# RWKV block inversion: each level product moves only 32 of 64 columns

## The reference, cut to what matters

```python
def step(S, inp):
    r_t, d_t, k_t, v_t, kk_t, a_t = inp
    sa = jnp.einsum('bhij,bhj->bhi', S, -kk_t)
    S = (S * d_t[:, :, None, :] + sa[..., None] * (kk_t * a_t)[:, :, None, :]
         + v_t[..., None] * k_t[:, :, None, :])
    return S, jnp.einsum('bhij,bhj->bhi', S, r_t)
```

## Time and profile before

| | |
|---|---|
| median of 3 runs | 2666.61 us (2660.39 to 2673.18) |
| profiled execution, time | 2664.87 us |
| its span | 2663.1 us |
| TensorE matmuls, busy | 2542.4 us, 95% |
| VectorE, busy | 1375.4 us, 52% |
| ScalarE, busy | 1082.2 us, 41% |
| GpSimd, busy | 1630.0 us, 61% |
| granted TensorE clock, mean | 0.976 |

### The profile page before, as it was taken

How to read it: one execution, slowest core, us unless ns; L and a number is a source line. 1 busy time by engine, 2 the same in 40 slices (tenths; PEclk the granted TensorE clock), 3 DMA queues, 4 the chain that set the end, 5 groups by cost and what they waited for, 6 DMA issues and landing times.

```text
span 2663.1 us, 56828 instructions
## 1 busy us (share of the span) xinstructions
PE 2542.4 (95%) x23437; PEld 2350.3 (88%) x23437; DVE 1375.4 (52%) x2444; ACT 1082.2 (41%) x1752; POOL 1630.0 (61%) x844
## 2 busy tenths in 40 slices
PE   5899999889979999999999999999989999999997
PEld 3799999657757999999999999999988888888887
DVE  0450355773336455995574010010177777777777
ACT  1333433341223434444333333333444554555555
POOL 0366677012225776888655777777667777777763
PEclk9899999889989999999999999999999999999999
DMA  9987845567855444445555654654588999999884
GB/s 374 395 290 268 274 170 171 183 249 251 261 194 218 170 165 140 158 159 180 180 176 193 239 196 159 257 194 168 192 309 307 323 374 321 332 358 318 311 305 131
DMA packets 213561, 639.92 MB, mean 240 GB/s; under 512 B 16520, under 2 KB 26264, under 8 KB 183832
## 3 DMA queue, kind: packets, MB, share of 16 engines
q1 hardware_dynamic: 176712, 514.54, 55.6%
q0 software_dynamic: 27472, 97.56, 10.1%
q10 hardware_dynamic: 9216, 25.53, 2.4%
HBM read 605.61 MB, written 31.97 MB: 239 GB/s over the span
## 4 chain that ended last, share of the span: by engine, by line
PE 69%; issue 12%; POOL 9%; DVE 5%; DMA 4%; ACT 1%; POOLq 0%; DVEq 0%; ACTq 0%; SPq 0%
PE bank L929 68%; POOL ring_lo L806 8%; DMA kept<-in_peer_v 3%; DVE ring_lo L2791 1%; DVE act_hl L2788 1%; ACT hi_peer L1690 0%; PE bank L932 0%; DVE staged L2853 0%; POOL ring_lo L813 0%; DMA staged<-in_w_ada 0%; DVE staged L2373 0%; DVE staged L2397 0%; ACT act_hl L1690 0%; ACT staged L1687 0%; DVE staged L2781 0%
## 5 line engine op out<-in xcount | busy, mean ns | idle before, releaser
L1690 ACT ACTIVATE hi_peer<-kept 128x1024 fp32r<-128x1024 f32 x544 | 559.2, 1053 | 906.2 <-PE bank L929 775.4
L806 POOL TENSOR_TENSOR ring_lo<-kept,hi_peer 128x1024 fp32r<-128x1024 f32 x288 | 718.1, 2516 | 271.5 <-ACT hi_peer L1690 271.5
L929 PE MATMUL bank<-h_hi,ring_lo 128*128 128x288 f32 x2848 | 839.5, 295 | 0.0
L929 PE MATMUL bank<-act_hl,hi_peer 128*128 128x416 f32 x2048 | 626.1, 371 | 10.5 <-DVE staged L2853 5.6
L929 PE MATMUL bank<-h_hi,hi_peer 128*128 128x288 f32 x2048 | 609.0, 297 | 2.8 <-POOL ring_lo L806 2.5
L929 PE MATMUL bank<-h_lo,hi_peer 128*128 128x288 f32 x2048 | 604.9, 295 | 0.0
L929 PEld LDWEIGHTS bank<-h_hi,ring_lo 128*128 128x128 f32 x2848 | 537.8, 189 | 0.0
L929 PE MATMUL bank<-act_hl,ring_lo 128*128 128x208 f32 x2048 | 529.5, 259 | 0.0
L929 PEld LDWEIGHTS bank<-act_hl,hi_peer 128*128 128x128 f32 x2048 | 385.8, 188 | 50.1 <-issue 37.9
L929 PE MATMUL bank<-staged 64*64 64x64 f32 (+12 forms) x6760 | 388.2, 300 | 37.6 <-issue 19.8
L2788 DVE TENSOR_TENSOR act_hl<-staged,act_hl 128x416 fp32r<-128x416 f32 x256 | 261.8, 1023 | 271.5 <-ACT act_hl L1690 271.0
(11 more groups left out here) (261 smaller groups left out, 3100.6 us busy)
## 6 DMA issues: line engine op xcount, KB each, us to landing
kept<-in_peer_u SPq DMA_DIRECT2D x128, 1024.0 KB, 4.8
kept<-in_peer_v SPq DMA_DIRECT2D x128, 1024.0 KB, 8.7
kept<-in_w_ada SPq DMA_DIRECT2D x64, 1024.0 KB, 8.8
kept<-in_w_in SPq DMA_DIRECT2D x50, 1024.0 KB, 4.9
staged<-in_w_ada SPq DMA_DIRECT2D x32, 1024.0 KB, 6.5
kept<-in_w_adaf SPq DMA_DIRECT2D x32, 1024.0 KB, 5.9
kept<-in_w_out SPq DMA_DIRECT2D x16, 1024.0 KB, 5.1
kept<-in_w_q SPq DMA_DIRECT2D x16, 1024.0 KB, 4.8
```

Source lines behind the costliest of these rows:

```text
L806: pool.tensor_tensor(ring_lo[:, n % RING_SLOTS, cols], ring[n % RING_SLOTS][:, cols], hi_slot(n)[:, cols].bitcast(F32), ALU.subtract).then ...
L929: return pe.matmul(out, lhsT, rhs, start=start, stop=stop)
L1690: return act.activation(out, in_, ACT.Copy)
```

## The change

At level i the joining part is nonzero only between an even block of 2^i tokens and the odd one after it. X has then nonzero columns only in even blocks, the product added to the inverse likewise, and the product added to the transpose only in odd ones. `block_half` picks these 32 of 64 columns (runs of 2^i at a distance of 2^(i+1)). The matmuls stream these alone, ScalarE copies these alone, VectorE adds these alone. The stationary operands stay whole: so rows of X x Tt that come from columns of X outside are masked away by a per-partition factor of 0 or 1 (`early`, a new constant column for each level in a gap of a block of constants), and X is set to zero once before the first use, on GpSimd ahead of the first pair's mask of level 1. The number of matmuls, copies and additions stays.

```diff
+    put(c1, CST1, "early", (s >> np.arange(LEVELS)[None, :]) % 2 == 0)
...
+        def block_half(v, level, e):
+
+            return v.rearrange("p (n e b) -> p n e b", e=2, b=1 << level)[:, :, e, :]
...
+                    if p == 0 and i == 1:
+                        pool.tensor_copy(X.rearrange("p h (t o) -> p (h t) o", o=1), over(prm("zero"), 1, AH * L))
...
-                def times(bank, q, lhsT, rhs):
+                def times(bank, q, lhsT, rhs, level, e):
                     for h in range(8 * q, 8 * q + 8):
                         for j in range(2):
-                            mm = matmul(ps[bank][PART[j], (h % 8) * L:(h % 8 + 1) * L], lhsT[PART[j], h, :], rhs[PART[j], h, :])
+                            mm = matmul(block_half(ps[bank][PART[j], (h % 8) * L:(h % 8 + 1) * L], level, e),
+                                        lhsT[PART[j], h, :], block_half(rhs[PART[j], h, :], level, e))
                     return mm
...
-                        times(q, q, mk[i % 2], Ti).then_inc(S("x_sum"), 1)
+                        times(q, q, mk[i % 2], Ti, i, 0).then_inc(S("x_sum"), 1)
...
-                                times(2 + q, q, Tt, X).then_inc(S("t_sum"), 1)
-                            times(q, q, X, Tt).then_inc(S("t_sum"), 1)
+                                times(2 + q, q, Tt, X, i, 0).then_inc(S("t_sum"), 1)
+                            times(q, q, X, Tt, i, 1).then_inc(S("t_sum"), 1)
...
-                        copy(X[:, 8 * q:8 * q + 8].rearrange("p h t -> p (h t)"), ps[q][:, :]).then_inc(S("x_copied"), 1)
+                        copy(block_half(X[:, 8 * q:8 * q + 8].rearrange("p h t -> p (h t)"), i, 0),
+                             block_half(ps[q][:, :], i, 0)).then_inc(S("x_copied"), 1)
...
+                def add_inverse(q, bank, level):
+                    own = heads(Ti, q, level, 0)
+                    tt(own, own, block_half(ps[bank][:, :], level, 0), ALU.add).then_inc(S("t_added"), 1)
+
+                def add_turned(q, level):
+                    own = heads(Tt, q, level, 1)
+                    stt(out=own, in0=block_half(ps[q][:, :], level, 1), scalar=cst1("early")[:, level:level + 1], in1=own,
+                        op0=ALU.mult, op1=ALU.add).then_inc(S("t_added"), 1)
...
-                    tt(heads(Tt, q), heads(Tt, q), heads(mk[0], q), ALU.add).then_inc(S("t_added"), 1)
+                    own = heads(Tt, q, 0, 1)
+                    tt(own, own, heads(mk[0], q, 0, 1), ALU.add).then_inc(S("t_added"), 1)
```

More of the change, by code:

```diff
@@ L64 @@
 CST1, CST1_N = columns([
-    ("fold", 4 * NS), ("fold2", 2 * NS), ("comp", 38), ("quad", 2), ("spare", CST1_FIRST - 6 * NS - 40), ("blk", P), ("level", LEVELS * L), ("both", 2 * L), ("eye", L), ("incl", P), ("slevel", 2 * SM), ("sboth", 2 * SM),
+    ("fold", 4 * NS), ("fold2", 2 * NS), ("comp", 38), ("quad", 2), ("early", LEVELS), ("spare", CST1_FIRST - 6 * NS - 40 - LEVELS), ("blk", P), ("level", LEVELS * L), ("both", 2 * L), ("eye", L), ("incl", P), ("slevel", 2 * SM), ("sboth", 2 * SM),
     ("seye", SM), ("sincl", SM), ("seq", NB), ("wreset", N), ("breset", N), ("mreset", N), ("sel", BH * P), ("seqcol", NB * SM)])
@@ L2461, in _, with heads @@
                            ps[g][:, :].rearrange("p (h x) -> p h x", h=4), over(both, 1, 4), ALU.mult).then_inc(S("gram_done"), 1)
[L2463 to L2468, removed]
+                def heads(a, q, level, e):
+                    return block_half(a[:, 8 * q:8 * q + 8].rearrange("p h t -> p (h t)"), level, e)
+                def add_inverse(q, bank, level):
[5 more added lines that the diff above has]
+                        op0=ALU.mult, op1=ALU.add).then_inc(S("t_added"), 1)
                 dve.wait_ge(S("eye_set"), p + 1)
@@ L2472, in _ @@
                 for q in range(2):
-                    tt(heads(Tt, q), heads(Tt, q), heads(mk[0], q), ALU.add).then_inc(S("t_added"), 1)
+                    own = heads(Tt, q, 0, 1)
+                    tt(own, own, heads(mk[0], q, 0, 1), ALU.add).then_inc(S("t_added"), 1)
                     dve.wait_ge(S("x_sum"), x_sums(p, 0, q))
-                    add_bank(Ti, q, q)
+                    add_inverse(q, q, 0)
                 if p == 0:
@@ L2481, in _ @@
                             dve.wait_ge(S("t_sum"), t_sums(p, i, q, 0))
-                            add_bank(Ti, q, 2 + q)
+                            add_inverse(q, 2 + q, i)
                         dve.wait_ge(S("t_sum"), t_sums(p, i, q, 1))
-                        add_bank(Tt, q, q)
+                        add_turned(q, i)
                     if p == 0 and i < 3:
```

## The result

The changed kernel takes 2697.29 us (median of 4 runs, 2674.96 to 2707.82), the kernel before 2667.98 us (4 runs, 2660.39 to 2673.18): ratio 1.0102, 95% interval 1.0078 to 1.0126, slower by 1%. Predicted were 2666 us, within 0.5% of before. Six more runs of it in a later session gave 2696.52 us (2684.19 to 2702.03), ratio 1.0103 [1.0077, 1.0128].

A forecast was written before the change was run, and what follows sets the result against it. TensorE was taken to bound the inversions. Profiled 2664.87 us, -0.5 for products and 0 for the rest, gave 2664.4; with 1.7 us from profiled run to median, 2666 us, 8-in-10 range 2648 to 2678.

The forecast's parts named there:

- What bounds the kernel: In the two block inversions the chain of waits is TensorE alone, only matmuls or "issue"; TensorE's matmul side 95% busy.
- the price of a record: In the inversions' products, the longer of load and stream holds a tile; a record stays at 28.2 to 29.5 ns.
- the sign given for it: In a level: 128 records at 3.8 to 3.95 us, LDWEIGHTS near 133 ns, the matmul's own latency falling.
- Copies, additions, zeroing, mask: On ScalarE, VectorE and GpSimd in the inversions: copies 0.39 us, additions 0.47 us, zeroing 1.03 us, all covered; 0 on the path.
- Strided operands and results: In the inversions, moving operands in strides costs 0, bounded by 3.8 us if level 0's 128 records double.
- The rule on PSUM's lines: Rival: strided results slow matmuls in PSUM; 2670 us if level 0 doubles, 2723 us if all records do; 3%.
- the floor of 25 ns for a small matmul: Rival for the inversions' records: about 25 ns start to start however small, from 29.5, 8.6 us gained, 2657 us; 4%.
- Weight tiles from memory: In the inversions DMA does not bound: a level uses two tiles in 7.89 us, one can start every 2.69 us.
- the sum's term for the products: TensorE's 1920 inversion records gain between 0 and 2.5 us, taken as 0.5 us.
- The clock falls: Rival: in the two inversions, each fifth of 85 us of work at 1.2 GHz costs 17 us; 2683 us; 9%.
- The stream-bound rival: Rival: in the inversions moving columns set the price; record 17.0 ns, level 5.5 us, 24 us gained, 2642 us; 12%.

The follow-up runs named there:

- half_stationary: The changed kernel with each inversion matmul loading 32 of its 64 stationary columns and the additions multiplied by zero: 2662.15 us, ratio 0.9989.
- wide_all: The changed kernel with all inversion products streaming 64 columns again, its narrow copies, additions, zeroing and mask kept: 2667.84 us, ratio 0.9996.
- blocks32: The kernel before, rewritten with four 32x32 diagonal tiles at levels 0 to 4 and only the off-diagonal block at level 5: 2720.86 us, ratio 1.0192.
- again: The changed kernel, unchanged, run once more in a later session: 2696.52 us, ratio 1.0103 to the kernel before.
- wide_t: The changed kernel with only the products with X streaming 64 columns again, mask x inverse still 32: 2668.48 us, ratio 0.9996.
- lull_after: The changed kernel plus 24 useless matmuls with 18 moving columns in level 0 of the first inversion: 2702.67 us, ratio 1.0131.
- the burst: The changed kernel plus four useless 128 x 512 matmuls between level 1's two product steps in the first inversion: 2680.76 us, ratio 1.0048.

## Why the prediction was wrong

*What bounds the kernel, and the price of a record: right.* The chain is TensorE. A record costs 29.1 ns for 29.5, because a 64-column load holds its tile as long as the 64 moving columns did; half_stationary, with 32 stationary columns, brings it to 15.9 ns. Of the sign given for it one part was wrong: the matmul's own duration did not fall (219 ns, as the 128 records of the same product before).

*Copies, additions, zeroing, mask: right.* wide_all keeps them all and takes the time of before. Additions take 0.42 and 0.48 us where I had 0.47 for all, copies 0.38 where I had 0.39.

*Strided operands and results: right, 0.* At level 0, single elements at a stride of two, 64 wide records of another product and the 64 narrow ones together take 3.92 us, as 128 do elsewhere:
```profile
597.99 3.92 PE L936 MATMUL bank<-staged 64*64 64x64 f32 x128
```
That alone would not exclude slower results: 32 columns at twice the 0.8 ns a column of the prediction, 51 ns, would still fit under the 59 ns for which the load holds a tile. In half_stationary the load is half as long, and level 0's strided records still cost (1.2 - 0.19)/63 = 16 ns, as those of level 1 do:
```profile
L936 PE MATMUL bank<-staged 64*32 64x32 f32 x64 | 1.2, 193 | 0.0
```
The rule on PSUM's lines that was weighed in the prediction (the Trainium skill, "SBUF — State Buffer", in its note on cachelines) is not borne out by these traces. Nor is the floor of 25 ns for a small matmul (the Trainium skill, "TensorE: Matmul & The Clock Gate", section "Wait — 56ns, not 53.3ns?"), for records on four tiles: 84 of them in 0.92 us in blocks32, (0.92 - 0.19)/83 = 8.8 ns, and 18 ns even for a program matmul, which leaves two. On two tiles 15.9 ns a record is 31.8 for a program matmul, which tells only if the floor is one of records.

*Weight tiles from memory: right.* No DMA became a wait.

*Where it failed: the sum's term for the products, -0.5 us, which priced every record at a granted clock of 1.00.* I did so because both inversions showed 1.00 in the one profile I had. In again the same records cost up to 1.8 times that (a level 14.25 us for 7.84), and the two stages lost 27.5 and 5.9 us. A clock that reads 1.00 tells what it was, not how firmly it was held. It is lost now and then with wide products too: in the kernel before itself (0.84 between 650 and 660 us, behind a gap of 2.14 us), in wide_all (0.96 between 650 and 690 us) and in wide_t's first inversion. In the changed kernel it fell behind the 18-column products or at a gap of 1.6 to 1.9 us. What the kernel before had, and the change took away, is the way back up; whether the change also makes falls more frequent was not tested.

That is my rival "The clock falls", with the right place and sign and part of the cause. Its chance of 9% was too small. Its size too: I allowed a fifth of the two stages' 85 us of work, 17 us, so 2683; in again it was all of the first inversion, 69 us as they passed, and some 10 in the second, for 33.4 us. The row I used against it, two dense weight tiles in each level, was no protection: they are in the stuck levels also.

And the row that spoke for it I read and put aside. The 18-column products at 820.8 us sat at 0.50 throughout, while being dense. Over 3.4 us that was a hint and no more, but it pointed at what the experiments found: records whose price is the load, with little moving behind them, did not bring the clock back.

*The stream-bound rival* (2642 us) would hardly have been had either. In half_stationary most of what shorter records gave went into "issue" gaps, 6 us left of 25.

*Left open.* Why the first inversion of the profiled run escaped the fall and that of again did not: the same products and the same 0.43 us gap stand ahead of both. With the longer lull of lull_after all four runs were slow alike. What exactly lifts the clock is known only from cases: wide products at either place did, the burst did, the 64x128 product did, and so did the bonus with a weight tile behind it. Narrow products behind 64-column loads did not, with two weight tiles a level; behind 32-column loads they did, in one profile.

No version that computes everything beat the kernel before; wide_all equals it, and its smaller copies and additions buy nothing.

## What to carry to other kernels

Halving what moves through TensorE saves nothing where the load of the stationary side is as long, and may cost the clock: ask of a dense stage not only whether its clock is 1.00, but what would bring it back after a lull. If a change of TensorE's operands is slower in some runs and not in others, look at the mean clock of each run before reading a profile; the profiled run may be the lucky one. Before making matmuls shorter, look for "issue" gaps in the stretch: they can take most of what shorter records give.

## What was not expected of the hardware

- The clock's level was not told by TensorE's busy time: 69 us at 1.2 GHz, with TensorE busy for 99% of the first 50 (49.57 us), ended by one product with 128 moving columns. The same narrow products ran at 2.4 GHz for the rest of the inversion behind a burst.
- Where the clock came back among narrow products in the second inversion, it did so at wide bonus matmuls with a weight tile straight behind them; with the two apart it stayed down for 68 us (one profile).
- Adding 5.6 us of useless dense matmuls made a kernel 16 us faster.
- At 1.2 GHz the 64x64 loads take longer too: LDWEIGHTS 223 ns for 135, 64 records in 3.63 us, not 2.06, and a level 14.25 us for 7.84.
- Records of 9 to 10 ns did not make a faster stretch: 1370 matmuls in 50 us, where the kernel before, with 29.5 ns, passes 1218; TensorE stood for 2 to 3 us between them, and the clock was at 0.74.
